# Two unread matrix products with activations as weights, ahead of one pass of the attention projection and one of the second FFN

## What is computed

```python
x = x + ml[5] * merge_branches(y_conv_l, o_l, gt_l, w_branch_conv, w_branch_attn, w_out)
#   merge_branches: (g_conv * (y_conv @ w_bc) + g_attn * (o_attn @ w_ba)) @ w_out
x = x + 0.5 * ml[8] * swiglu(modulate(rms_norm(x, norm3_g), ml[6], ml[7]), ffn2_w_in, ffn2_w_out)
#   swiglu: a, b = split(h @ w_in); (silu(a) * b) @ w_out
```

## Time and profile before

| | |
|---|---|
| median of 3 runs | 1337.68 us |
| the three runs | 1337.42, 1337.68, 1344.29 us |
| span of the profiled execution, first to last instruction | 1343.2 us |
| own time of the profiled execution | given by its span alone |
| TensorE busy with products | 1312.1 us, 98% of the span, 9320 products |
| VectorE, ScalarE busy | 903.8 us (67%), 645.0 us (48%) |
| mean granted TensorE clock | 0.991 of 2.4 GHz |

### The profile page before, as it was taken

The page is one execution under the profiler, slowest core; times in us unless marked ns, Lnnn a source line. Parts: engine busy times, 40 slices in busy tenths (PEclk is TensorE's granted clock), DMA queues, the critical chain, the costliest instruction groups (busy, mean ns, idle before and its releaser), DMA issues. The chain is left out here.

```text
span 1343.2 us, 23450 instructions
## 1 busy us (share of the span) xinstructions
PE 1312.1 (98%) x9320; PEld 1214.2 (90%) x9320; DVE 903.8 (67%) x1461; ACT 645.0 (48%) x1026; POOL 27.3 (2%) x27
## 2 busy tenths in 40 slices
PE   5999999999999999999999999999999999999998
PEld 3688888888889999999999999998999999999998
DVE  3577875556558497755775555678887666689873
ACT  4432222222336335545554445566666766556553
POOL 0000000000020000000000000200000000100000
PEclk6999999999999999999999999999999999999999
DMA  8746556464554345444545655565556445536660
GB/s 304 262 161 200 190 188 217 160 233 163 190 178 142 111 137 162 137 147 135 180 145 186 199 172 171 164 188 154 155 149 188 142 141 185 162 110 205 207 202 32
DMA packets 201484, 230.20 MB, mean 171 GB/s; under 512 B 7072, under 2 KB 191648, under 8 KB 201376
## 3 DMA queue, kind: packets, MB, share of 16 engines
q1 hardware_dynamic: 201088, 228.42, 53.8%
q10 hardware_dynamic: 288, 0.28, 0.1%
HBM read 227.63 MB, written 1.05 MB: 170 GB/s over the span
## 5 line engine op out<-in xcount | busy, mean ns | idle before, releaser
L1048 PE MATMUL P<-XHB,WH 128*128 128x256 f32 (+1 forms) x1808 | 556.0, 308 | 7.6 <-DVE XLB L1707 3.7
L1049 PE MATMUL P<-XLB,WH 128*128 128x256 f32 (+1 forms) x1808 | 546.0, 302 | 0.0
L1050 PE MATMUL P<-XHB,WL 128*128 128x256 f32 (+1 forms) x1808 | 545.9, 302 | 0.0
L1911 DVE TENSOR_TENSOR WL<-W,WH 128x1024 fp32r<-128x1024 f32 x358 | 431.9, 1225 | 89.9 <-ACT WH L1490 89.7
L1490 ACT ACTIVATE WH<-W 128x1024 fp32r<-128x1024 f32 x358 | 368.8, 1041 | 251.2 <-PE P L1050 162.3
L1048 PEld LDWEIGHTS P<-XHB,WH 128*128 128x128 f32 x1808 | 340.9, 189 | 28.1 <-issue 7.3
L1050 PEld LDWEIGHTS P<-XHB,WL 128*128 128x128 f32 x1808 | 342.2, 189 | 14.8
L1049 PEld LDWEIGHTS P<-XLB,WH 128*128 128x128 f32 x1808 | 340.6, 188 | 15.3 <-issue 0.5
L1048 PE MATMUL P<-GH,WH 128*128 128x256 f32 (+1 forms) x372 | 122.1, 328 | 0.0
L1049 PE MATMUL P<-GL,WH 128*128 128x256 f32 (+1 forms) x372 | 121.5, 327 | 0.0
L1050 PE MATMUL P<-GH,WL 128*128 128x256 f32 (+1 forms) x372 | 121.5, 327 | 0.0
(11 more groups left out here) (314 smaller groups left out, 1791.4 us busy)
## 6 DMA issues: line engine op xcount, KB each, us to landing
W<-in_ffn_w_in SPq DMA_DIRECT2D x88, 512.0 KB, 4.8
W<-in_w_in_ab SPq DMA_DIRECT2D x72, 512.0 KB, 4.7
W<-in_w_modt SPq DMA_DIRECT2D x56, 512.0 KB, 3.8
W<-in_w_in SPq DMA_DIRECT2D x52, 512.0 KB, 3.7
W<-in_ffn_w_out SPq DMA_DIRECT2D x40, 512.0 KB, 4.6
W<-in_w_in_c SPq DMA_DIRECT2D x32, 512.0 KB, 4.4
W<-in_w_mod SPq DMA_DIRECT2D x16, 512.0 KB, 7.4
W<-in_w_out_ab SPq DMA_DIRECT2D x16, 512.0 KB, 4.3
```

Of the source, the lines that this page charges most:

```text
L1048: pe.matmul(o, h[:, k, c], xh[:, kk, a:b], start=kk == 0, stop=False)
L1049: pe.matmul(o, h[:, k, c], xl[:, kk, a:b], start=False, stop=False)
L1050: mm = pe.matmul(o, l[:, k, c], xh[:, kk, a:b], start=False, stop=kk == gm.nk - 1)
L1911: dve.tensor_tensor(l, a, h.bitcast(F32), ALU.subtract).then_inc(S["wl"], 1)
```

## The change

`gemm` gets an argument `unread` and hands it to the first part of the pass; the first half of that part carries it as `c`. For k below `c` the function `chunk` then makes two more products ahead of the others, behind the same wait for WL: activations stand (128 tokens of the high and of the low part of block k) and 256 columns of weights stream (low and high part of the same block). Both write bank 4 of PSUM, with start and stop set, and nothing reads them. `unread` is 1 for pass i = 1 of ma and for the pass of fb2 with f = 2, so that four products are added in all.

```diff
-    def gemm(self, kind, i, wt, r0, nk, c0, cols, turned=True, g=0, first=False, norm=False):
+    def gemm(self, kind, i, wt, r0, nk, c0, cols, turned=True, g=0, first=False, norm=False, unread=0):
...
-                self.part(gm, k0, m, j, norm)
+                self.part(gm, k0, m, j, norm, unread if k0 == 0 else 0)
...
-        self.step("ck", gemm=gm, k0=k0, nk=m, chunk=j, half=0)
+        self.step("ck", gemm=gm, k0=k0, nk=m, chunk=j, half=0, c=unread)
...
-            self.gemm("ma", i, w["w_branch_attn"], 0, 8, 256 * i, (0, T), first=i == 0)
+            self.gemm("ma", i, w["w_branch_attn"], 0, 8, 256 * i, (0, T), first=i == 0, unread=int(i == 1))
...
-                self.gemm(f"fb{n}", f, win, 0, 8, DFF + f * 128, cols)
+                self.gemm(f"fb{n}", f, win, 0, 8, DFF + f * 128, cols, unread=int(n == 2 and f == 2))
...
                 pe.wait_ge(S["wl"], s.chunk + 1)
+                for k in range(s.c):
+                    pe.matmul(P[:, 4, 0:256], xh[:, k, a:a + 128], l[:, k, :], start=True, stop=True)
+                    pe.matmul(P[:, 4, 0:256], xl[:, k, a:a + 128], h[:, k, :], start=True, stop=True)
```

More of the change, by code:

```diff
@@ L224, in tiles_of, with part @@
             self.tile_free.append(self.freed(gm))
-    def part(self, gm, k0, m, j, norm=False):
+    def part(self, gm, k0, m, j, norm=False, unread=0):
         kind = gm.kind
```

## The result

| | before | changed |
|---|---|---|
| median of 14 runs each | 1338.11 us | 1344.14 us |
| range | 1337.35 to 1344.78 us | 1342.49 to 1349.70 us |
| ratio | | 1.0033, 95% interval 1.0018 to 1.0047 |
| profiled execution: time, span | span 1343.2 us | 1349.70, 1347.4 us |
| products in the profile | 9320 | 9324 |

The change makes the kernel slower, by 0.33% in the ratio, which here comes out as that of the means, and by 6.0 us in the medians. Seven of these lie at 1342.5 to 1343.9 us, six at 1344.4 to 1345.0 and one at 1349.7.

A forecast was written before the change was run, and what follows sets the result against it. TensorE was taken to bound the kernel; -1.43 - 6.31 + 0.46 + 0.02 = -7.26 us gave 1335.9 from the profiled span, the projections' gain alone 1336.7 from the median, so 1336.3 us was forecast, range 1330.0 to 1343.5 us.

The forecast's parts named there:

- What bounds the kernel, and the two paces: TensorE, busy 98% of the span, bounds the kernel; same-shape products go at 117.8 or 113.4 ns, 4.4 ns apart.
- wide: The slower TensorE pace, 117.8 ns a product, read in the second FFN and the attention and output projections.
- tight: The faster TensorE pace, 113.4 ns a product, read at the program's end and in the even layer's projection.
- The four products at 0.46 us: The added unread products stand on TensorE's path and cost 4 x 0.115 = 0.46 us; bounds nothing to 1.2 us.
- What follows the pair in the projections: The 324 products behind the pair in ma and res turn wide to tight, gaining 1.43 us; otherwise 0.
- What follows the pair in the second FFN: The 1,434 products behind the pair turn wide to tight, gaining 6.31 us against the profiled execution.
- the pair turns tight into wide: Rival: an FFN arriving tight leaves its pair wide, paying 6.3 us: 1343.0 us, or 1344.5; chance 0.20.
- The four seams in the trace: Clean places where activations standing give way to weights standing: three turned wide to tight, at 902.0 tight to wide.
- the sum: All terms against the profiled execution's span of 1343.2 us: -7.26 us, giving 1335.9 us.
- What is late next: In the second FFN at the tight pace, ScalarE and VectorE keep up; loads and splitting cost nothing.
- the third case: Rival: the FFN is tight ahead of its pair and wide behind it, 1343.0 or 1344.5 us; chance 0.20.
- the fourth rival: Two products do nothing to the pace at either place; their cost is 0.5 us: 1338.2 us; chance 0.15.

The follow-up runs named there:

- e2: Changed kernel without the pair in the attention projection, so only the second FFN's pair is left: 12 runs, 1342.98 to 1345.23 us, ratio 1.0006.
- e8: Changed kernel without the projection pair, and the pair in reversed order ahead of each of 20 second-FFN passes: one execution, 1349.36 us.
- e10: Changed kernel without the projection pair, and two pairs in a row ahead of each of 20 second-FFN passes: one execution, 1354.11 us.
- e1: Changed kernel without the second FFN's pair, so only the attention projection's pair is left: 9 runs, 1335.41 to 1338.84 us, ratio 0.9950.
- e13: e1 once more, on another chip: 12 runs, median 1344.30 us, 3 of them below 1341 us.
- e12: Kernel before plus one unread product ahead of pass 1 of ma: 10 runs, median 1336.52 us, ratio 0.9995.
- e9: Kernel before plus one unread product in ma, and a pair then one product in second FFN and program end: median 1337.58 us, ratio 0.9984.

## Why the prediction was wrong

It gave 1336.3 us and no change; measured were 1344.14 us and slower.

- *What bounds the kernel, and the two paces.* Right. Every stretch shown in which TensorE did not wait went at one of them (112 to 113.4 or 117.2 to 117.8 ns by the windows), and where the pace went, the time went. That the FFN settles by chance is borne out: up to the FFN's first seam the kernel before, e2 to e8 and e10 issue the same products, and four of these nine profiles reached it wide and five tight. That the median of the kernel before is of executions with a tight FFN fits the times of other kernels' profiles, but none of the kernel before at 1338 us was taken: e1 and e13 have it tight in spans of 1336.9 and 1334.8 us, e12 and the kernel before wide in 1341.0 and 1343.2 us.
- *The four products at 0.46 us.* Right in size: a pair takes 0.23 us in the timeline above.
- *What follows the pair in the projections.* Wrong. "Wide to tight gives 1.43 us" was not given by a pair; changed kernel, e1 and e13 all stay at 117.6 ns. Its other end, 0, is what happened. One product would have done it, for 0.12 us (e12, e9).
- *What follows the pair in the second FFN.* This step failed with the consequence. The forecast was that "behind the pair the tight pace is the usual one". A pair leaves it wide from either pace, so the executions that would have been tight, which set the median, pay 1,434 x 4.4 ns = 6.3 us. Measured were 6.0 us between the medians and 6.6 us, with the pair, between the FFNs of e1 and e2. The rival "the pair turns tight into wide" had the place, the direction and the price (1343.0 us, or 1344.5 with nothing won in the projections, against 1344.14), with a chance of 0.20. Its mechanism, an exchange, is that of one or three products, not of two: under it the executions that arrive wide, four of 14 by the kernel before, would have come out tight, and none of 14 did.
- *Where the inference broke.* The four seams in the trace had 48 or 24 products ahead of them, and the change has two. I carried the rule over, with doubt only about whether two are enough to act. And of the four seams, the one that bore on a tight arrival (902.0) went tight to wide; the forecast needed the opposite of it.
- *A span beside times.* The 1343.2 us of the profiled execution are a span, and 1337.68 us is a time. The changed kernel's profiled execution has a time of 1349.7 us at a span of 1347.4, e13's 1336.88 at 1334.8. So the sum's 1335.9 us is a span and belongs to a time of some 1338 us, and 1336.3, halfway between it and 1336.7, mixes the two. This is 1 us at most of the 8 that were missed.
- *What is late next.* Right: at 113.3 ns in e1 and e9 TensorE does not stand still; VectorE is busy for 93.6 of 158 us.
- *The range*, to 1343.5 us, had the third case's better half only. The corner of no gain in the projections with the FFN lost, written out at 1344.5 us, was left outside it.
- *One pace only*, the fourth rival's premise, is contradicted by every window here, with 113.3 and 117.7 ns for one shape at one clock. The Trainium skill (TensorE: Matmul & The Clock Gate, "Back-to-back issue gap") gives the formula behind 109 ns for isolated products only, and says that in a stream with weight loads both set the distance; it has no value for 256 columns. So it did not speak for a single pace as the prediction had it.

## What to carry to other kernels

Where TensorE hardly ever stands still and the time still jumps between runs, compare the number of products per microsecond between stretches of the same shape before looking for a wait: busy shares and the clock tell nothing of it. A state seen to turn at one kind of place is not a rule for another kind, so put the planned perturbation at twenty places of one kernel and read its table of transitions from one profile before building on it. And when the kernel before has several levels, take its shares in the same rounds as the change, and fix the state rather than compare medians.

## What the runs showed of the hardware that was not expected

- Products of 128x128 by 256 columns, back to back, operands of type fp32r, have two stable distances at the granted clock 1.00: 113.3 and 117.8 ns. Nothing that the profiles show of the granted clock, the DMA share or the waits was seen to go with them.
- The number of products with activations standing, put between two runs with weights standing, goes with what follows: one or three exchange the distances, two leave the wide one from either; four were met wide only, and left it wide. Whether it is the number or the kind of these products was not parted. Two products of the usual kind change nothing at the tight pace (20 of 20).
- At the start of the second FFN, where TensorE still waits for other engines, the same products settled at 117.8 ns in four profiles and at 113.3 ns in five. What in the hardware holds the two distances was not found.
